# The first modulation matrix of a two-block transformer kernel: ten more of its sixteen chunks multiplied on TensorE in column groups, with VectorE left the copies

## What is computed

```python
def ada_terms(cond, w_mod, b_mod):
    m = jax.nn.silu(cond) @ w_mod + b_mod        # (1024,) @ (1024, 6144)
    return jnp.split(m, 6, axis=-1)
...
for layer in range(2):
    sh1, sc1, gt1, sh2, sc2, gt2 = ada_terms(c, w_mod[layer], b_mod[layer])
    a = modulate(rms_norm(h, g_mix_pre[layer]), sh1, sc1)
    if layer == 0:
        csh1, csc1, ... = ada_terms(c_ctx, w_mod[layer], b_mod[layer])
        ac = modulate(rms_norm(ctx, g_mix_pre[layer]), csh1, csc1)
        y = hybrid_mixer(a, ac, ...)             # projections, 5-tap convolutions, gated delta rule, attention
    else:
        y = conformer_conv(a, ...)
    h = h + gt1 * rms_norm(y, g_mix_post[layer])
    f = swiglu_ffn(modulate(rms_norm(h, g_ffn_pre[layer]), sh2, sc2), ...)
    h = h + gt2 * rms_norm(f, g_ffn_post[layer])
```

## Time and profile before

| | us |
|---|---|
| median of 3 runs (1646.6 to 1647.88) | 1646.93 |
| the profiled execution, whole time | 1645.11 |
| its span in the trace | 1643.3 |
| TensorE busy (matmuls) | 1455.4 |
| VectorE busy | 964.5 |
| ScalarE busy | 505.4 |
| GpSimd busy | 230.5 |
| mean granted TensorE clock | 0.947 of full speed |

### The profile page before, as it was taken

The page is one execution under the profiler, slowest core; times in us unless marked ns, Lnnn a source line. Parts: engine busy times, 40 slices in busy tenths (PEclk is TensorE's granted clock), DMA queues, the critical chain, the costliest instruction groups (busy, mean ns, idle before and its releaser), DMA issues. The chain is left out here.

```text
span 1643.3 us, 20885 instructions
## 1 busy us (share of the span) xinstructions
PE 1455.4 (89%) x8014; PEld 1179.6 (72%) x8014; DVE 964.5 (59%) x1634; ACT 505.4 (31%) x858; POOL 230.5 (14%) x224
## 2 busy tenths in 40 slices
PE   3899288488788999989998999978988999989997
PEld 2357245388784999978856999966665678669997
DVE  1348956688773655556966555546675224265665
ACT  2110245244203443340035344331120222154443
POOL 0000603755300000012100000023342000000000
PEclk9999679699999899999999999999998999999999
DMA  7547320134405455423215555512222233345551
GB/s 309 225 180 286 120 77 1 38 116 155 164 16 212 157 188 191 179 83 132 74 39 192 192 186 179 179 57 91 95 110 77 77 116 114 117 157 194 186 180 75
DMA packets 24659, 226.66 MB, mean 138 GB/s; under 512 B 2705, under 2 KB 2833, under 8 KB 4242
## 3 DMA queue, kind: packets, MB, share of 16 engines
q1 hardware_dynamic: 23040, 220.31, 36.8%
q10 hardware_dynamic: 1554, 5.47, 0.9%
HBM read 224.72 MB, written 1.05 MB: 137 GB/s over the span
## 5 line engine op out<-in xcount | busy, mean ns | idle before, releaser
L1815 DVE TENSOR_TENSOR arena_r<-ring,arena_r 128x1024 fp32r<-128x1024 f32 x196 | 229.7, 1222 | 181.3 <-ACT arena_r L1362 181.3
L725 PE MATMUL psum<-aT,ring 128*128 128x256 f32 (+1 forms) x1216 | 309.7, 413 | 3.7 <-ACT aT L1317 2.2
L725 PEld LDWEIGHTS psum<-aT,ring 128*128 128x128 f32 x1216 | 233.0, 194 | 76.7 <-issue 48.1
L801 PE MATMUL psum<-aT_r,arena_r 128*128 128x256 f32 x920 | 260.0, 283 | 0.7 <-DVE arena_r L1815 0.7
L803 PE MATMUL psum<-aT_r,arena_r 128*128 128x256 f32 x920 | 260.4, 283 | 0.0
L802 PE MATMUL psum<-aT_r,arena_r 128*128 128x256 f32 x920 | 260.3, 283 | 0.0
L1362 ACT ACTIVATE arena_r<-ring 128x1024 fp32r<-128x1024 f32 x196 | 194.8, 1051 | 193.8 <-PE psum L841 164.1
L841 PE MATMUL psum<-arena_r 128*128 128x512 f32 x912 | 220.6, 391 | 0.0
L841 PEld LDWEIGHTS psum<-arena_r 128*128 128x128 f32 x912 | 166.6, 188 | 31.6
L801 PEld LDWEIGHTS psum<-aT_r,arena_r 128*128 128x128 f32 x920 | 176.3, 192 | 3.6 <-issue 0.9
L802 PEld LDWEIGHTS psum<-aT_r,arena_r 128*128 128x128 f32 x920 | 176.3, 192 | 2.7
(11 more groups left out here) (377 smaller groups left out, 1765.7 us busy)
## 6 DMA issues: line engine op xcount, KB each, us to landing
ring<-in_w_ffn SPq DMA_DIRECT2D x44, 1536.0 KB, 6.6
ring<-in_w_mod SPq DMA_DIRECT2D x32, 1536.0 KB, 7.8
ring<-in_w_ff SPq DMA_DIRECT2D x32, 1024.0 KB, 4.8
ring<-in_w_in_g SPq DMA_DIRECT2D x8, 1536.0 KB, 6.4
ring<-in_w_conf_i SPq DMA_DIRECT2D x8, 1024.0 KB, 4.8
ring<-in_w_hyb_f SPq DMA_DIRECT2D x4, 1536.0 KB, 7.1
ring<-in_w_in_a SPq DMA_DIRECT2D x4, 1536.0 KB, 6.7
ring<-in_w_in_b SPq DMA_DIRECT2D x4, 1536.0 KB, 6.3
```

The costliest lines, as they stand in the source:

```text
L725: last = mm(bank(use)[:, out_at:out_at + rhs(k).shape[1]], weights[:, k * P:(k + 1) * P], rhs(k), start=(k == 0), stop=(k == KT - 1))
L801: mm(into, hi, x_hi[:, k, :], start=(k == 0), stop=False)
L1815: tt(w_lo[j % 2][:, at], slot(c)[:, at], w_hi[j % 2][:, at].bitcast(F32), ALU.subtract).then_inc(split_ready, 1)
```

## The change

All sixteen chunks of mod0 take the way of chunks 0 to 5. `mod_sums(0, j)` becomes `mod_copy(j)` at the same places of VectorE's program, and `mod0(j)` on TensorE becomes the columns of one chunk and the product of the next. The buffers `macs` go, `mod_ev` moves to another place in SBUF (its old place is written by the token-side projections), slots with mod0 chunks are freed by TensorE's `ring_used`, and the rest of the modulation terms waits for all sixteen groups of columns.

```diff
--- before.py
+++ after.py
@@ -58,7 +58,7 @@
 MOD_C = 384
 NMOD = 6 * D // MOD_C
 MOD_CTX = 6
-MOD0_PE = tuple(range(MOD_CTX))
+MOD0_PE = tuple(range(NMOD))
 
 SUMS = {key: n for n, key in enumerate([(0, j) for j in range(NMOD) if j not in MOD0_PE]
                                        + [(1, j) for j in range(NMOD)])}
@@ -297,7 +297,7 @@
         _u = USE[_name][_j]
     elif _name == "branch":
         _u = USE[_name][4 * _j + 3]
-    elif _j == _chunks - 1:
+    elif _j == _chunks - 1 and _name != "mod0":
         _u = USE["y", {"hyb_o": 0, "conf_o": 2, "out2": 4}[_name]][0]
     else:
         _u = None
@@ -407,7 +407,7 @@
             at, n = CONST_AT[name]
             return consts[:, at:at + n]
 
-        macs, mod_ev = view(yT_t, 0, 4, MOD_C), view(z_t, 0, 2, MOD_C)
+        mod_ev = view(yT_t, 0, 2, MOD_C)
         mod_acc, mod_out = psum[:, 3584:3584 + MOD_C], psum[:, 3968:4064]
         macs1 = ring[:, 2 * SLOT:2 * SLOT + 6 * D]
         ident, ones = const("ident"), const("ones")
@@ -708,14 +708,6 @@
                     last = mm(mod_out[:, 2 * n:2 * n + 2], mod_ev[:, j % 2, b * P:(b + 1) * P], sel, start=True, stop=True)
                 last.then_inc(mod_sel, 1)
 
-            def mod0(j):
-                n = SUMS[0, j]
-                pe.wait_ge(sums_ready, n + 1)
-                for b in range(3):
-                    at = 2 * (3 * j + b)
-                    last = mm(mod_out[:, at:at + 1], macs[:, n % 4, b * P:(b + 1) * P], ones[:, 0:1], start=True, stop=True)
-                last.then_inc(mod_mm, 1)
-
             def feature_block(use, weights, rhs, out_at=0, fresh=()):
 
                 for k in range(KT):
@@ -887,7 +879,9 @@
                                          fresh=() if 3 * c + b else (0, 1))
                     filled(last, use)
                 if c:
-                    mod0(MOD_CTX + c - 1)
+                    if c > 1:
+                        mod_columns(MOD_CTX + c - 2)
+                    mod_products(MOD_CTX + c - 1)
 
 
             uses = iter(USE["hyb_t"])
@@ -901,9 +895,12 @@
                         last = mm(bank(use)[:, 0:HYB_TC], aT[:, k, tile * P:(tile + 1) * P],
                                   wt[:, k * HYB_TC:(k + 1) * HYB_TC], start=(k == 0), stop=(k == KT - 1))
                     filled(last, use)
-                mod0(MOD_CTX + c + 3)
-            for j in range(MOD_CTX + 7, NMOD):
-                mod0(j)
+                mod_columns(MOD_CTX + c + 2)
+                mod_products(MOD_CTX + c + 3)
+            for j in range(MOD_CTX + 6, NMOD):
+                mod_columns(j)
+                if j + 1 < NMOD:
+                    mod_products(j + 1)
 
 
             pe.wait_ge(att_rope, 1)
@@ -1659,9 +1656,7 @@
 
                 if layer == 0:
                     src = mod_out.rearrange("p (n c) -> p n c", c=2)
-                    dve.wait_ge(mod_sel, MOD_CTX)
-                    if 5 in vectors:
-                        dve.wait_ge(mod_mm, SUMS[0, NMOD - 1] + 1)
+                    dve.wait_ge(mod_sel, NMOD if 5 in vectors else MOD_CTX)
                 b = col("b_mod")[:, 48 * layer:48 * layer + 48]
                 m = modT[:, layer, :, :]
                 early, late = 0 in vectors, 5 in vectors
@@ -1707,19 +1702,9 @@
             def mod_steps(layer, j):
 
                 n = SUMS[layer, j]
-                if layer:
-                    chunk = slot(j % 2)
-                    dve.wait_ge(mod1_loaded[j % 2], 16 * (j // 2 + 1))
-                    if j == 0:
-                        dve.wait_ge(sums_ready, n)
-                    todo = [(macs1[:, j * MOD_C:(j + 1) * MOD_C], 0, MOD_C)]
-                else:
-                    c = CHUNK["mod0", j]
-                    chunk = slot(c)
-                    dve.wait_ge(ring_ready[c % SLOTS], 16 * (c // SLOTS + 1))
-                    todo = [(macs[:, n % 4, :], 0, MOD_C)]
-                    if n >= 4:
-                        dve.wait_ge(mod_mm, n - 3)
+                chunk = slot(j % 2)
+                dve.wait_ge(mod1_loaded[j % 2], 16 * (j // 2 + 1))
+                todo = [(macs1[:, j * MOD_C:(j + 1) * MOD_C], 0, MOD_C)]
                 for k in range(KT):
                     if k:
                         dve.wait_ge(mac, mac_n[0])
@@ -1867,7 +1852,7 @@
                     norm_evac(i, (kp,))
 
             for j in range(MOD_CTX, MOD_CTX + 4):
-                mod_sums(0, j)
+                mod_copy(j)
             taps = col("hyb_conv").rearrange("p (b k) -> p b k", k=CONV_A)
             for grp in range(3):
                 n = 2 if grp < 2 else 1
```

## The result

The changed kernel has a median of 1661.28 us (9 runs, 1659.72 to 1669.5); the kernel before, run beside it, 1647.45 (9 runs, 1643.31 to 1656.22). The ratio is 1.0086, with a 95% interval of 1.0063 to 1.0108: 0.9% slower. The prediction was 1663.5 us.

The account below looks back on a forecast made before the run. Everything up to the first attention maximum was taken to hang on the attention-squares reduction, moved from 182.65 to 199.3 by in-line products, the held convolution group and the copy tail: 1646.9 + 16.6 = 1663.5 us, range 1657 to 1669.

Parts of the forecast that it names:

- Products in line: TensorE before the handover: six products at 1.50 us less 0.59 delay the last projection block by 8.4 us, to 180.4.
- the bounds 1.31 and 1.82: Price of one product between projection blocks: 1.31 us four groups side by side, 1.82 with a drained pipe before and behind.
- The held group: VectorE: third convolution group waits behind copies 12 and 13, starts at 186.0 and ends at 193.9, where today it ends at 170.92.
- the wait for copy 11 costs nothing: VectorE: copy 11 holds the second convolution group until 162.9, free because that group ends near 176, before TensorE's 180.4.
- The tail: After the third group, copies 14 and 15 at TensorE's low clock end at 199.3, after GpSimd's squares at 198.1; reduction +16.6 us.
- Loads at nothing: Projection loads queued behind modulation chunks land in 9.4 us, needed after 10.9; 1.5 us margin, so no cost.
- The rest as a mere shift: Everything behind the reduction is the same program, so its 16.6 us delay should reach the end whole.
- (a): TensorE drains at each change of tiling mode: 0.32 us more per product, 2.2 in all, 1665.7 us; chance 0.09.
- (b): A token-side load lands last behind a 1.5 MB chunk: at 13 us per pair 6.3 more, 1669.8 us; chance 0.06.
- (c): TensorE's column groups run one behind another, 5.24 us per product in place of 1.50: above 1689 us; chance 0.02.
- (d): VectorE's wait costs little, third group is ready early, only products count: +4.2 us, 1651.1; chance 0.05.
- (e): Third group free and products almost free on TensorE: reduction 4.3 us earlier, 1642.7 us; chance 0.04.

Follow-up runs that it names:

- thin: Changed kernel with the products of chunks 6 to 11 each cut to one matmul over 32 of 384 columns; 1656.45 us, ratio 1.0046 to the kernel before.
- twice: Changed kernel with the products of chunks 6 to 11 issued twice; 1674.81 us over 4 executions, ratio 1.0145 to the kernel before.
- conv3_early: Changed kernel with the third convolution group moved ahead of copies 12 and 13 on VectorE; 1663.95 us, ratio 1.009 to the kernel before.
- thin_conv3: Changed kernel with third convolution group ahead of copies 12 and 13 and products of chunks 6 to 11 cut; 1650.16 us, ratio 0.9991 to the kernel before.
- hybrid2: Kernel before with only chunks 14 and 15 moved to TensorE, square root before gate activations, third sum spread over attention maxima; 1638.63 us, ratio 0.9941.

## Why the prediction was right

**Products in line.** 8.4 us predicted for the end of the last projection block, 8.2 measured. The price was 1.50 each and is 1.43 (of the bounds 1.31 and 1.82 the lower was nearer), while a group of columns with the selector costs 0.65 in line where the group with ones cost 0.59. Part of the hit is luck: the products came out 0.4 us cheaper than forecast and the first 96 records 0.2 shorter, five groups of columns cost 0.3 more and the blocks 0.1. `thin` and `twice` show that it is per product and reaches the reduction.

**The held group.** Predicted start of the third group: 186.0 on the clock of the trace before; measured 184.67, which is 185.8 on that clock (53.01 - 51.86 = 1.15 more). The copies stand 2.94 us apart, as taken from the early chunks. `conv3_early` prices the holding at 5.9 to 6.3 us. That the wait for copy 11 costs nothing was right only because the third group was held: in `conv3_early` and `thin_conv3` the path to the reduction runs through the second group.

**The tail.** Predicted: low clock, 5.4 us from the end of the group to the reduction, the squares not last. Measured: 192.55 to 197.85, 5.3. The squares took 3.2 (2.46 + 0.76), not 4.2; VectorE, which summed chunk 14 beside them before, does one copy beside them now. That changed nothing, they were not last. Reduction predicted at 199.3, measured 199.0 on that clock. Counted from the end of the first 96 records the shift is 16.6 us.

**Loads at nothing.** Right for the changed kernel, no projection block waits. But the margin of 1.5 us was too large. From 97.01 to 106.2 us are 9.2 us, not 9.4, and the end of a transfer in the stretches comes before the landing that a block waits for: in `thin` the last pair is down to 31 GB/s in 154 to 155 us, and the block that waits for it starts at 155.36. In the changed kernel a token-side load takes 9.3 us from its own issue (median of 4), which is 0.4 behind the first of its pair, so 9.7, and it is needed after 10.8: 1.1 us. In `thin`, which takes 1.25 us out of each block, a pair needed 10.3 and the last block waits.

**The rest as a mere shift.** 16.35 us in the stage, +14.6 in the spans, 13.8 between the medians; by the ratio 14.2, with 10 to 18 by its interval. 1.15 of the gap to the spans is the earlier start of that execution. The other 0.6 lies in five late stages that change by up to 2.4 us either way and nearly cancel: 185.2 to 183.7, 55.7 to 58.1, 34.3 to 35.7, 59.0 to 57.4, 142.6 to 141.2. "I see nothing that could except the clock" was the right reserve; that these stages nearly cancel in the two profiled executions is luck. What the prediction lacked is that an execution of the same kernel can lie 8 us from the next, as the range of its own runs of before (1646.6 to 1647.88) did not show.

**Rivals.** (a): entering and leaving cost 0.14 us per product, about 1 us in all, and the product with it still costs 1.43, less than the 1.50 of the forecast. (b): no wait. (c): the groups run side by side between full blocks. (d) and (e): both fell with the held group. The price of (d) was wrong too: with the group moved ahead the reduction is 10.0 us later than before, not 4.2, since copy 11 holds the second group and the chain of four copies stands behind the third.

## What to carry to other kernels

Moving work off an engine is worth what of it lies on the path. Of the ten sums eight were hidden beside the projections and two were not; moving the two gained, moving the eight loaded the engine that had no gap. A copy that waits for another engine holds all that stands behind it in program order: put independent work ahead of it, not behind. When the late engine is relieved, look for who is next (here ScalarE's table load, or the load of the third chunk) before the gain is counted. And read a gain in a second profile of the same kernel before you explain it: of 13.0 us at the end of the attention 7.2 were gone in the next one.

## What was not expected of the hardware

- The same program takes one of several whole times, 1646 or 1656 us for the kernel before (of the 25 executions beside `conv3_early`, 15 lie between 1643.7 and 1648.2 and 9 between 1655.8 and 1656.7). For the kernel with the early group a profile at each value shows stages at another granted clock; for the kernel before only one was taken, so there the cause is not shown. Differences under 10 us need the stage's own distances from the profile, or many executions.
- Keeping TensorE busy for 21 us did not carry over a pause of 5.63 us: four transposes took 1.11 us behind it, 0.66 at the high clock.
- Two executions of `hybrid2` ran the same first attention at different clocks, 1.00 and 0.50 in 208 to 216 us, behind the same idle time of 21.8 us for the rotation; the end of the attention lies 7.2 us apart.
- Leaving and entering a column-grouped product between full blocks costs 0.14 us together, on a product of 1.29.
- VectorE's sum of a chunk takes 4.96 us alone and 10.9 (1.76 + 9.10) beside GpSimd's rotation in the changed kernel, 10.8 in the kernel before.
